# Program's beginning: half of the modulation products on TensorE, early loads in other storage, two units with their low weights last, bias rows later

## The reference, cut to what matters

```python
c_act = jax.nn.silu(c)                              # c: [1, 1024]
mod = (c_act @ w_ada + b_ada)[:, None, :]           # w_ada: [1024, 6144]
sh1, sc1, g1, sh2, sc2, g2 = jnp.split(mod, 6, axis=-1)
h = rmsnorm(x, norm1_w) * (1 + sc1) + sh1
u = h @ w_in                                        # w_in: [1024, 5632]
```

## Time and profile before

| | us |
|---|---|
| median of 3 runs | 1684.8 (1683.87 to 1691.77) |
| the profiled execution's own time | 1684.51 |
| its span | 1682.7 |
| TensorE matmul busy | 1567.5 (93%) |
| VectorE busy | 930.2 (55%) |
| ScalarE busy | 624.3 (37%) |
| GpSimd busy | 49.8 (3%) |

### The profile page before, as it was taken

How to read it: one execution, slowest core, us unless ns; L and a number is a source line. 1 busy time by engine, 2 the same in 40 slices (tenths; PEclk the granted TensorE clock), 3 DMA queues, 4 the chain that set the end, 5 groups by cost and what they waited for, 6 DMA issues and landing times.

```text
span 1682.7 us, 19021 instructions
## 1 busy us (share of the span) xinstructions
PE 1567.5 (93%) x7519; PEld 1072.6 (64%) x7519; DVE 930.2 (55%) x1401; ACT 624.3 (37%) x904; POOL 49.8 (3%) x66
## 2 busy tenths in 40 slices
PE   2899998999899998999989998999988999999996
PEld 2777787888778787788878774333336876433332
DVE  5888687865578978755467864111006786211002
ACT  2354544434344464444335742111114573111111
POOL 2000000000000000000030200000000110000000
PEclk8899999999999999999989998999998998999998
DMA  9677555976567734765565337999995417799995
GB/s 340 220 249 245 185 177 179 318 259 225 190 232 256 271 126 152 274 209 176 190 162 188 101 128 302 410 409 409 409 371 176 153 51 267 305 409 408 409 409 215
DMA packets 149980, 427.66 MB, mean 254 GB/s; under 512 B 8120, under 2 KB 16560, under 8 KB 149888
## 3 DMA queue, kind: packets, MB, share of 16 engines
q1 hardware_dynamic: 146208, 417.43, 67.8%
q0 software_dynamic: 3456, 8.87, 1.8%
q10 hardware_dynamic: 224, 0.07, 0.0%
HBM read 425.30 MB, written 1.05 MB: 253 GB/s over the span
## 4 chain that ended last, share of the span: by engine, by line
PE 62%; DVE 17%; DMA 7%; SPq 7%; ACT 4%; issue 3%; DVEq 0%; ACTq 0%
PE gp L2341 26%; PE gp L2788 9%; PE gp L2564 9%; SPq L756 6%; PE gp L2807 4%; DVE wlo L1424 4%; DMA raw<-in_w_in 3%; PE mp L2828 2%; DMA raw_deep<-in_exp_w_up 2%; PE gp L2773 2%; ACT whi L872 2%; DMA raw_deep<-in_w_ada 2%; DVE acc L1296 1%; DVE ft L1485 1%; PE mp L2625 1%
## 5 line engine op out<-in xcount | busy, mean ns | idle before, releaser
L1424 DVE TENSOR_TENSOR wlo<-raw,whi 128x2048 fp32r<-128x2048 f32 (+1 forms) x131 | 287.2, 2193 | 171.0 <-ACT whi L872 168.8
L872 ACT ACTIVATE whi<-raw 128x2048 fp32r<-128x2048 f32 (+1 forms) x131 | 240.0, 1835 | 297.3 <-PE gp L2341 162.7
L2341 PE MATMUL gp<-whi,xt_hi 128*128 128x512 f32 (+1 forms) x792 | 313.9, 396 | 16.7 <-DVE xt_lo L1495 7.4
L2341 PE MATMUL gp<-whi,xt_lo 128*128 128x512 f32 (+1 forms) x792 | 305.0, 385 | 0.0
L2341 PE MATMUL gp<-wlo,xt_hi 128*128 128x512 f32 (+1 forms) x792 | 304.7, 385 | 0.0
L2341 PEld LDWEIGHTS gp<-whi,xt_hi 128*128 128x128 f32 x792 | 151.0, 191 | 54.7 <-issue 14.4
L2341 PEld LDWEIGHTS gp<-whi,xt_lo 128*128 128x128 f32 x792 | 150.7, 190 | 30.2
L2341 PEld LDWEIGHTS gp<-wlo,xt_hi 128*128 128x128 f32 x792 | 151.0, 191 | 27.6 <-issue 1.0
L2196 DVE TENSOR_SCALAR pr<-slots,key,dg 128x128 f32<-128x128 f32 x64 | 19.3, 343 | 255.2 <-PE gp L2818 255.2
L1296 DVE SCALAR_TENSOR_TENSOR acc<-raw,cact,acc 128x1024 f32<-128x1024 f32 x69 | 88.5, 1282 | 2.6 <-DMA raw<-in_w_ada 1.1
L2210 DVE TENSOR_TENSOR pr<-pr,gp 64x512 f32<-64x512 f32 x32 | 21.7, 679 | 123.3 <-ACT pr L1214 123.3
(11 more groups left out here) (443 smaller groups left out, 2476.1 us busy)
## 6 DMA issues: line engine op xcount, KB each, us to landing
raw<-in_w_in SPq DMA_DIRECT2D x60, 1024.0 KB, 5.8
raw<-in_w_ada SPq DMA_DIRECT2D x42, 1024.0 KB, 5.3
raw_deep<-in_exp_w_gate SPq DMA_DIRECT2D x28, 1024.0 KB, 16.2
raw_deep<-in_exp_w_up SPq DMA_DIRECT2D x28, 1024.0 KB, 14.9
raw_deep<-in_exp_w_down SPq DMA_DIRECT2D x28, 1024.0 KB, 15.0
raw<-in_w_gate SPq DMA_DIRECT2D x20, 1024.0 KB, 5.1
raw<-in_w_up SPq DMA_DIRECT2D x20, 1024.0 KB, 5.2
raw<-in_w_down SPq DMA_DIRECT2D x20, 1024.0 KB, 5.0
```

The costliest lines, as they stand in the source:

```text
L872: act.activation(halves1(s, l, units, cols)[0], slot(raw, g % RAW, units, cols), ACT.Copy).then_inc(hi_done.sem, 1)
L1424: dve.tensor_tensor(lo, slot(raw, g % RAW, units, cols), hi.bitcast(F32), ALU.subtract).then_inc(raw_read[g % RAW].sem, 1)
L2341: mm = pe.matmul(gp[:, q % 2, t, 0:wide], a[:, chunk, ts], w[:, unit, c0:c0 + wide], start=first and n == 0 and m == 0, stop=last and n == ...
```

## The change

The early ada units 3 to 8 go to a new array `ada_ahead`, which shares its storage with `u`, `gl` and `qt` (first written after the first products), so ScalarE's wait for `acc_done` 2 ahead of `split(0)` falls away. VectorE now does only units 0, 1 (vector 0) and 4, 5 (vector 1), with unit 1 ahead of `mean_square`. Units 2, 3, 6 and 7 are multiplied by TensorE directly, in `sum_mod`: the 128x128 block of the unit is the stationary operand, a column of `cact` the moving one, 8 column blocks x 2 row chunks = 16 float32 matmuls of one column for each unit. `sum_mod(0)` goes ahead of the transposes of `xn2`. `take_mod` of vectors 0 and 1 adds three partial columns instead of one. The first two products run over all hi·hi and lo·hi pairs first and over hi·lo (with `wlo`) last, so that they begin on ScalarE's `hi_done`; on VectorE `low_bank(1)` goes ahead of `split(0)`. GpSimd loads the bias rows of layer 0 only after `acc_done` 2.

```diff
+        ahead = ExitStack()
+        ada_ahead = sb("ada_ahead", [P, 2 * ADA + 1 - RAW, UNITS], ctx=ahead)
+        ahead.close()
...
-            part = raw[:, n] if n < RAW else raw_deep[:, n - RAW]
+            part = raw[:, n] if n < RAW else ada_ahead[:, n - RAW]
...
+        EARLY_ACC = (0, 1, ADA, ADA + 1)
...
-                pool.wait_ge(*x_final.at(l, 0))
+                if l == 0:
+                    pool.wait_ge(*acc_done.at(0, 2))
+                else:
+                    pool.wait_ge(*x_final.at(l, 0))
...
-                    act.wait_ge(*acc_done.at(0, 2))
                     split(0)
...
+                        if l == 0 and vec < 2:
+                            m = modc[:, vec, :]
+                            lk(dve.tensor_tensor(m, gp[:, 0, vec, 0:KD], pcol[:, l, KD * vec:KD * (vec + 1)], ALU.add))
+                            lk(dve.tensor_tensor(m, gp[:, 0, vec, KD:2 * KD], m, ALU.add))
+                            dve.tensor_tensor(m, gp[:, 1, vec, 0:KD], m, ALU.add).then_inc(mod_taken.sem, 1)
+                            return
...
+                    early_ada(EARLY_ACC[1])
                     for t in range(NT):
                         mean_square(0, t)
                     for t in range(NT):
                         rsqrt(NORM1 + t, t, t + 1)
-                    for n in range(1, 2 * ADA):
+                    for n in EARLY_ACC[2:]:
                         early_ada(n)
...
                     low_bank(0)
+                    low_bank(1)
                     split(0)
-                    low_bank(1)
...
+                    if early_sum:
+                        for i in (2, 3):
+                            n = ADA * vec + i
+                            cols = gp[:, 0, vec, KD:2 * KD] if i == 2 else gp[:, 1, vec, 0:KD]
+
+                            pe.wait_ge(early_in[n], 16)
+                            for c in range(KD):
+                                for k in range(2):
+                                    mm = pe.matmul(cols[:, c:c + 1], early(n)[:, k, P * c:P * (c + 1)],
+                                                   cact[:, 2 * i + k:2 * i + k + 1], start=k == 0, stop=k == 1)
+                            if n < RAW:
+                                mm.then_inc(raw_read[n].sem, 1)
...
+                def product_low_last(s):
...
+                    pe.wait_ge(*hi_done.at(l, s + 1))
...
+                    for m, pairs in enumerate((((a_hi, w_hi), (a_lo, w_hi)), ((a_hi, w_lo),))):
+                        if m == 1:
+                            pe.wait_ge(*raw_read[g % RAW].at(l, g // RAW + 1))
...
                 if l == 0:
+                    pe.wait_ge(zeroed, 2)
+                    sum_mod(0, 0)
                     pe.wait_ge(*xn_ready.at(l, 2))
                     for b in range(4):
                         turn(b, xn2, 2 * P * b).then_inc(tr_done.sem, 1)
-                    pe.wait_ge(zeroed, 2)
-                    sum_mod(0, 0)
                     sum_mod(1, 0)
                     pe.wait_ge(*mod_taken.at(0, 2))
...
-                        product(s)
+                        product_low_last(s)
```

More of the change, by code:

```diff
@@ L1396, in early_ada @@
                     vec, i = divmod(n, ADA)
+                    earlier = (*EARLY_ACC, 2 * ADA).index(n)
                     dve.wait_ge(early_in[n], 16)
@@ L1411, in early_ada @@
                     ins.then_inc(early_read, 1)
-                    dve.wait_ge(early_read, n + 1)
+                    dve.wait_ge(early_read, earlier + 1)
                     if n < RAW:
                         dve.sem_inc(raw_read[n].sem, 1)
-                    if i == ADA - 1:
+                    if n + 1 in (2, ADA + 2):
                         dve.sem_inc(acc_done.sem, 1)
@@ L1446, in take_mod @@
                         c = MOD_COL[vec]
-                        src = gp[:, 0, vec, 0:KD] if l == 0 and vec < 2 else mp[:, MOD_BANK[vec], c:c + KD]
+                        if l == 0 and vec < 2:
[4 more added lines that the diff above has]
+                            return
+                        src = mp[:, MOD_BANK[vec], c:c + KD]
                         dve.tensor_tensor(modc[:, vec, :], src, pcol[:, l, KD * vec:KD * (vec + 1)], ALU.add).then_inc(mod_taken.sem, 1)
@@ L2306, in sum_mod @@
                 else:
-                    bank = gp[:, 0, vec, :] if l == 0 and vec < 2 else mp[:, MOD_BANK[vec % 6], :]
+                    early_sum = l == 0 and vec < 2
+                    bank = gp[:, 0, vec, :] if early_sum else mp[:, MOD_BANK[vec % 6], :]
                     c0 = MOD_COL[vec % 6]
@@ L2354, in product @@
                     return mm
+                def product_low_last(s):
+                    g = G_OF["split", s]
+                    _, units, cols = weights(("split", s), l)
+                    w_hi, w_lo = halves1(s, l, units, cols)
+                    (q, c0, wide, parts, first, last, name), = group_jobs(s)
+                    a_hi, a_lo = stationary[name]
+                    pe.wait_ge(*hi_done.at(l, s + 1))
+                    if first:
+                        pe.wait_ge(*pair_free[q % 2].at(l, 2 * (q // 2)))
+                    for m, pairs in enumerate((((a_hi, w_hi), (a_lo, w_hi)), ((a_hi, w_lo),))):
+                        if m == 1:
+                            pe.wait_ge(*raw_read[g % RAW].at(l, g // RAW + 1))
+                        for t in range(NT):
+                            ts = slice(P * t, P * (t + 1))
+                            for n, (unit, chunk) in enumerate(parts):
+                                for i, (a, w) in enumerate(pairs):
+                                    mm = pe.matmul(gp[:, q % 2, t, 0:wide], a[:, chunk, ts], w[:, unit, c0:c0 + wide],
+                                                   start=first and m == 0 and n == 0 and i == 0,
+                                                   stop=last and m == 1 and n == len(parts) - 1)
+                    mm.then_inc(w_used.sem, 1)
                 def turn_tile(t):
```

## The result

The changed kernel takes 1706.64 us in the median of 5 runs (1702.17 to 1709.45); the kernel before, run beside it, 1689.02 (1683.87 to 1694.04). The ratio is 1.0098, 95% interval 1.0077 to 1.0119: slower by 1.0%, 16.5 us on the 1684.5 of the profiled execution (13 to 20). The direction and the place were forecast; the time lies 9.6 us above the 1697.0 forecast and above the range of 1683.5 to 1702.

The account below looks back on a forecast made before the run. A start-up, bound by loads, VectorE and TensorE in turn, then a long run of matmuls; modulation ends at 56.35 instead of 43.85, +12.5 us, rest 0: 1684.5 + 12.5 = 1697.0. Own range 1693.5 to 1701.5; 8 in 10: 1683.5 to 1702.

Parts of the forecast that it names:

- What bounds the start, and that it passes through: Start-up before the first product: loads, VectorE, TensorE bound it in turn; what delays or advances it reaches the program's end.
- The loads: Early ada loads: with the bias rows later, units 2 to 7 land 2.7 us earlier, unit 7 at 34.6, unit 1 at 18.0.
- TensorE's term: Modulation sums on TensorE: 7.1 us a unit against 2.6 on VectorE, ending at 59.75 instead of 43.85 at the lower level.
- the 3.4 us given back behind the transposes at the full level: After the 16 transposes TensorE runs about 3.4 us at clock 1.00, so the modulation ends at 56.35, not 59.75.
- the three adds: `take_mod(1)` becomes three linked adds of about 0.2 us, 0.4 more, which fits into a slack of 0.5.
- the bounds of unit 1: Landing of ada unit 1, taken as 18.0, bounds 16.7 to 19.4: 1.4 us either way.
- the reordering: Order of splits on VectorE behind the modulation: 0, with bounds of 2.3 us lost and 1.6 gained.
- The case at 1700.4: No stretch at clock 1.00 behind the transposes: 15.9 us slower; lower level with or without the stretch had 0.64 together.
- The order of the splits at nothing: `low_bank(1)` ahead of `split(0)` starts products about 2.0 us sooner, but TensorE then waits for unit 3: 0 gained.
- Raised clock: Rival: one-column matmuls raise TensorE's clock themselves, 0.24 us each; modulation ends at 43.85, 1684.5, no change; chance 0.21.
- held clock: Rival: one-column matmuls cannot raise the clock but hold what the transposes raised; +8.0 us, 1692.5; chance 0.11.

Follow-up runs that it names:

- the rows alone: The kernel before with only the bias rows of layer 0 loaded later, when both accumulators are complete: ratio 0.9982 (0.9964 to 1.0).
- the products alone: The kernel before with only units 2, 3, 6, 7 on TensorE and the new storage: ratio 1.0073; a second, single execution took 1709.14 us.
- one unit: Unit 3 alone on TensorE, against a version with all units on VectorE, later bias rows and early rotary angles: ratios to the kernel before 1.0048, 1.0022.
- the low weights last alone: The kernel before with new storage, no ScalarE wait before its first split, low weights of units 0 and 1 last: ratio 1.0005 (0.9993 to 1.0017).
- the unused matmuls: All units on VectorE, later bias rows, early rotary angles, plus unit 3's matmuls on TensorE, result unread: ratio to the kernel before 1.0035 (1.0011 to 1.0059).

## Why the prediction came out as it did

**What bounds the start, and that it passes through: right.** Unit 3 is split 16.6 us later, and the ratio says 16.5.

**The loads: right in size but for unit 1.** Unit 7 lands at 34.8 (34.6 forecast), 2.5 sooner. Unit 1 gains 0.1, near the bound of nothing, where I took 1.4. So `sum_mod(0)` starts at 22.29, not 20.6. The run with the rows alone shows the gain that VectorE would have had: 2.4 us at its last unit.

**TensorE's term: right in size and mechanism.** 7.1 us for a unit were forecast, 6.83 measured from start to start; the end without any stretch at the full level was put at 59.75 and is at 59.85, because 80 matmuls of 0.427 instead of 0.443 (I had divided a duration with its last tail by eight) make up 1.3 us of the late start, and the transposes 0.2. Without this term the loss is gone (ratio 0.9999). Not priced was that putting `sum_mod(0)` ahead of the transposes starts the series 2 us later than the other order.

**The step that failed: the 3.4 us given back behind the transposes at the full level.** I took one trace's stretch at 1.00 behind the transposes for a rule. In the changed kernel's trace none came: the eight sums behind the transposes took 3.41 us, and 1.9 would have been the sign. (It is one trace of five executions; the other four left none.) The kernel with the products alone showed one execution with it and one without. Of the 16.0 us by which the modulation ends later, this term had given back 3.4. Without it the sum reads 1700.4, which the text had as its other end.

The Trainium skill, page "TensorE: Matmul & The Clock Gate", section "Part 4: PE-mode transpose", says that the full clock does not engage for transposes. I set this aside for one row. The traces bear out neither: the 1.92 us of sums right behind the transposes in one execution speak against the rule, the 3.41 in the other for it. Of all 13 traces six record a stretch at 1.00 behind the transposes and seven record none.

**The range.** The bounds as given add up to 1694.0 and 1700.7 about 1697.0, not to the 1693.5 and 1701.5 of the text, which is little. 1684.5 + 15.9 and 0.4 for the three adds is 1700.8; the measured median is 1706.6. Of the 5.8 between them some 4.5 are the base: the kernel before took 1689.0 beside the changed one, and 1684.5 in the execution that I built on. The 1.3 left are less than the ratio's interval can tell (13 to 20 us). The upper end of 1702 was too narrow by the prediction's own numbers. The case at 1700.4 with the bounds of unit 1 (1.4) and of the reordering (2.3) on top already gives 1704.1, and three runs of the kernel before spread over 8 us (1683.87 to 1691.77).

**The order of the splits at nothing: right.** Alone it gives a start 1.95 us sooner, and TensorE waits 1.65 for unit 3. In the changed kernel the same wait is there, 1.60 us ahead of unit 3.

**The rivals.** Raised clock (0.21) and held clock (0.11) are both out: 37.6 us of one-column matmuls and transposes without a gap raised nothing, and a full level there at the start was lost in the middle of them. The Trainium skill, same page, section "What's actually happening", has it that "activity releases the throttle"; the traces here don't bear that out for every activity: TensorE busy for 4.00 of 4.00 us went with 0.50.

## What to carry to other kernels

Before work is moved to an engine that looks idle, multiply the instructions by their time from a row of the same shape and lay them in series: a one-column float32 matmul with 128x128 weights cost TensorE 0.43 us at the lower level, so a 1 MB unit takes 7 us there and 2.6 on VectorE. Half of the work became far more than half of the time. When an engine does become the bound, put the work that is ready first at the head of its list. A gain on one side of a handover (products that start 2 us sooner) is worth nothing while the other engine's list is the bound; shorten that list instead. And build a range on the spread of the runs shown as well as on the terms of the sum, and look at a gain at the start in the whole program's time too.

## What the runs showed of the hardware

- One-column matmuls keep TensorE busy and still lose it the full level: 1.84 us for 16 records, then 6.96 for 32, with no gap between them.
- A record of a one-column matmul takes as long as one of a transpose with 128 columns: in the changed kernel's trace 16 of the first take 3.40 us from start to start (from 22.29) and 16 of the second 3.45 (from 39.34), both at the lower level.
- Behind sixteen float32 transposes a stretch at the full level comes in some executions only. Of six traces with one-column matmuls within about 1 us behind them, two show the double pace (1.92 us for 16 records: the first with the products alone, the second with one unit) and four don't (3.41 to 3.55). Of all 13 traces six show the stretch, and in three of these (the kernel before, the rows alone, the low weights last alone) TensorE stood idle for 7 to 8 us, did the transposes and nothing right behind them. I have no row that tells which it will be.
- The runs of one kernel, where there are 12 or more, spread over 9 to 18 us (1680.5 to 1696.6 for the kernel before in 29 runs, 1681.7 to 1699.6 for the unused matmuls in 12). The mean level between 1300 and 1460 us is 0.93 in some traces and 0.99 in others; such differences come far behind the start that was changed.
- The granted-clock column says 1.00 until the first change of level that the trace holds. Ahead of that, the distance between records is the only witness, and a run's mean clock takes that time at 1.00, whatever it was.
